# Where a latent attention phase places the gate-projection matmuls that fill its heads

## The reference

```python
q = split_heads(rms_norm(c_q, mla_cq_norm) @ mla_w_uq, MLA_HEADS)          # 8 heads
kv = split_heads(rms_norm(c_kv, mla_ckv_norm) @ mla_w_ukv, MLA_HEADS)
...
q = rms_norm(q, mla_q_norm)                      # per head and token
k = rms_norm(k, mla_k_norm)
... # rope on the last 32 of 96 columns
o_mla = merge_heads(block_causal_attention(q, k, v)) @ w_branch_mla
g_fox, g_mla = jnp.split(jax.nn.sigmoid(gate_logit + b_gate), N_BRANCH, axis=-1)
```

## Time and profile before

| | us |
|---|---|
| median of three runs | 2499.22 |
| the profiled execution | 2498.03 |
| span of its profile | 2496.2 |
| PE busy in the span | 2379.8 (95%) |
| DVE busy | 1411.5 (57%) |
| ACT busy | 960.2 (38%) |
| POOL busy | 505.1 (20%) |

### The profile page before, as it was taken

The page is one execution under the profiler, slowest core; times in us unless marked ns, Lnnn a source line. Parts: engine busy times, 40 slices in busy tenths (PEclk is TensorE's granted clock), DMA queues, the critical chain, the costliest instruction groups (busy, mean ns, idle before and its releaser), DMA issues. The chain is left out here.

```text
span 2496.2 us, 36863 instructions
## 1 busy us (share of the span) xinstructions
PE 2379.8 (95%) x14060; PEld 2108.6 (84%) x14060; DVE 1411.5 (57%) x2057; ACT 960.2 (38%) x1621; POOL 505.1 (20%) x632
## 2 busy tenths in 40 slices
PE   7999999999977999999999999989999999999999
PEld 7999999999977888887788888868877888887887
DVE  8665555665554674672555555454386666556553
ACT  6333333343333454453344333353343333333331
POOL 0033200000022432440233333332301232000000
PEclk8999999999988999989999999999999999999999
DMA  5366633375421000001111111034514665327553
GB/s 193 138 206 202 209 119 107 145 274 182 158 84 53 27 2 26 26 1 36 38 50 38 42 37 37 31 118 160 202 59 139 229 212 192 131 72 295 203 198 104
DMA packets 132698, 297.99 MB, mean 119 GB/s; under 512 B 10096, under 2 KB 57072, under 8 KB 129216
## 3 DMA queue, kind: packets, MB, share of 16 engines
q1 hardware_dynamic: 132544, 295.88, 34.1%
HBM read 206.99 MB, written 88.72 MB: 118 GB/s over the span
## 5 line engine op out<-in xcount | busy, mean ns | idle before, releaser
L1079 DVE TENSOR_TENSOR f_w_lo<-f_rw,f_w_hi 128x1024 fp32r<-128x1024 f32 x154 | 194.9, 1265 | 222.1 <-ACT f_w_hi L591 222.1
L842 PE MATMUL f_ps<-u_hi,f_w_hi 128*128 128x260 f32 (+1 forms) x1056 | 280.6, 320 | 10.6 <-DVE u_lo L1017 10.4
L842 PE MATMUL f_ps<-u_lo,f_w_hi 128*128 128x260 f32 (+1 forms) x1056 | 280.3, 320 | 0.0
L842 PE MATMUL f_ps<-u_hi,f_w_lo 128*128 128x260 f32 (+1 forms) x1056 | 279.9, 320 | 0.0
L842 PE MATMUL f_ps<-f_far_hi,f_w_hi 128*128 128x260 f32 (+1 forms) x792 | 214.3, 325 | 18.6 <-DVE f_ev L1095 8.8
L591 ACT CAST f_w_hi<-f_rw 128x1024 fp32r<-128x1024 f32 x154 | 160.9, 1046 | 163.5 <-PE f_ps L842 159.6
L842 PE MATMUL f_ps<-f_far_hi,f_w_lo 128*128 128x260 f32 (+1 forms) x792 | 213.0, 324 | 0.0
L842 PE MATMUL f_ps<-f_far_lo,f_w_hi 128*128 128x260 f32 (+1 forms) x792 | 212.7, 323 | 0.0
L842 PEld LDWEIGHTS f_ps<-u_hi,f_w_hi 128*128 128x128 f32 x1056 | 175.9, 190 | 26.0 <-issue 11.5
L842 PEld LDWEIGHTS f_ps<-u_lo,f_w_hi 128*128 128x128 f32 x1056 | 175.6, 189 | 14.0
L842 PEld LDWEIGHTS f_ps<-u_hi,f_w_lo 128*128 128x128 f32 x1056 | 175.7, 189 | 13.7
(11 more groups left out here) (392 smaller groups left out, 5964.1 us busy)
## 6 DMA issues: line engine op xcount, KB each, us to landing
f_rw<-in_gu SPq DMA_DIRECT2D x88, 512.0 KB, 4.2
f_rw<-kept_dsum SPq DMA_DIRECT2D x32, 704.0 KB, 4.4
f_rw<-kept_hid SPq DMA_DIRECT2D x33, 520.0 KB, 5.6
f_rw<-in_down SPq DMA_DIRECT2D x24, 704.0 KB, 4.2
f_rw<-kept_hid SPq DMA_DIRECT2D x33, 512.0 KB, 5.7
h_in<-in_wd SPq DMA_DIRECT2D x11, 1024.0 KB, 6.7
kept_dsum<-h_in SPq DMA_DIRECT2D x44, 256.0 KB, 2.9
h_out<-in_wd SPq DMA_DIRECT2D x11, 1024.0 KB, 7.3
```

Of the source, the lines that this page charges most:

```text
L842: last = nc.tensor.matmul(out[:, b, 0:N], w[:, c], u[:, b * N:(b + 1) * N], start=(j < 3 and k == 0 and i == 0), stop=(k == 3 and i == 2), ...
L1079: nc.vector.tensor_tensor(slot(w_lo, st), src, slot(w_hi, st).bitcast(F32), ALU.subtract).then_inc(wlo_done, 1)
```

## The change

Three tables and one condition change.

- `GROUPS`, used for the seven heads prepared beside another: place 1 of step 6 had 3 groups and has 1; place 0 of steps 8 and 9 had none and has 1 each.
- `FIRST`, the first head: place 1 of step 5 had 3 groups and has 1; place 0 of steps 11 and 13 had none and has 1 each. The copy of the last logit tile (`COPY_FIRST`) moves from step 12 to 13 with the last group.
- `first_roots`: the `split_lo` of the last unit comes in step 6 where it came in step 8.

```diff
         GROUPS = {(w, x): 1 for w in range(14) for x in range(2)}
-        GROUPS.update({(0, 1): 2, (1, 1): 2, (3, 1): 2, (4, 1): 2, (11, 1): 2, (12, 1): 2, (13, 0): 0, (13, 1): 0,
-                       (6, 1): 3, (8, 0): 0, (9, 0): 0})
+        GROUPS.update({(0, 1): 2, (1, 1): 2, (3, 1): 2, (4, 1): 2, (11, 1): 2, (12, 1): 2, (13, 0): 0, (13, 1): 0})
...
-        FIRST.update({(-1, 0): 1, (-1, 1): 4, (0, 0): 1, (0, 1): 2, (5, 0): 1, (5, 1): 3})
+        FIRST.update({(-1, 0): 1, (-1, 1): 4, (0, 0): 1, (0, 1): 2, (5, 0): 1, (5, 1): 1})
         FIRST.update({(w, x): 1 + 2 * x for w in range(1, 5) for x in range(2)})
-        FIRST.update({(w, 0): 1 for w in (8, 9, 10, 12)})
+        FIRST.update({(w, 0): 1 for w in range(8, 14)})
...
-        COPY_FIRST = (0, 2, 4, 12)
+        COPY_FIRST = (0, 2, 4, 13)
...
-                if 1 <= w < NU:
+                if 1 <= w <= NU:
                     split_lo(0, 0, w - 1)
-                if w == MAXIMA_FROM:
-                    split_lo(0, 0, NU - 1)
```

## The result

| | before | after |
|---|---|---|
| median, us (6 runs each) | 2499.53 | 2515.23 |
| range, us | 2498.03 to 2505.18 | 2508.69 to 2521.39 |
| profiled execution, us | 2498.03 | 2510.72 |
| its span, us | 2496.2 | 2508.9 |

The changed kernel is slower: ratio 1.0055, 95% interval 1.0039 to 1.0072, so about 14 us (15.7 between the medians). The direction was forecast, the size (7.7 us) was half of it, and the median lies above the range of 2500.5 to 2511.5.

The account below looks back on a forecast made before the run. PE, busy 95% of the span, was taken as the bound. Steady heads 6.3 us plus first head 1.4 made 7.7, giving 2505.7 on the profiled execution, 2506.9 on the median; forecast 2506.3 us, range 2500.5 to 2511.5.

Parts of the forecast that it names:

- Step 6 costs a wait of what left it: Steady heads, step 6: two groups leave, PE waits about 1.3 us for POOL's unchanged chain, step only 0.05 us earlier.
- The wait in step 9 goes: Steady heads, step 9: the arriving group covers the maxima tile's wait on DVE, gaining 0.44 us a head.
- Per steady head 0.90: Seven steady heads: 1.39 - 0.05 - 0.44 = 0.90 us more each, 6.3 us in all.
- The first head's order, 1.35: First head: 0.91 us from later DVE reductions plus 0.44 from the step 11 group delay transpose and next scores by 1.35.
- the forecast's 1209.56 and 1218.0: First head: predicted starts of the second wave of tiles, near 1209.56, and of the transpose, near 1218.0.
- The step 13 group: First head, step 13: the group lies in the 0.72 us wait before the transpose, costing nothing; 0.70 if uncovered.
- Rival 1: Steady heads, step 6: POOL's Newton steps finish sooner, so the sum is 1.5 to 4.6 us, about 2501.5; chance 0.10.
- Rival 2: Not slower: the chain into step 6's broadcast ends 1.24 us sooner; 2.9 us less than before, about 2495.7; chance 0.06.
- nothing is won or lost up to here: First head's last broadcast: it already waited 0.29 us for POOL; two groups fewer only lengthen that wait, at no cost.
- rival 3: Steady heads: PE's clock falls to 1.2 GHz after step 6's wait, about 3.5 us more each, 25 us, 2531; chance 0.04.
- its 0.91 us of order: First head: with `split_lo` ahead, DVE's maxima reductions start near 1209.22, 0.91 us later, and the delay runs through.

Follow-up runs that it names:

- both fillers: Changed kernel plus two unused product triples ahead of the first head's last broadcast and two ahead of its third maxima tile; 2507.31 us, ratio 1.0035.
- its filler: Changed kernel plus one unused triple ahead of the last head's first scores and one ahead of its first 512-column weighted sum; 2514.41 us, ratio 1.0057.
- once more: The changed kernel measured again with nothing altered; 2516.24 us, ratio 1.0059.
- first-head edits alone: Kernel before with only `FIRST`, `COPY_FIRST` and the early `split_lo` changed, old `GROUPS` kept; 2509.85 us, ratio 1.0038.
- late split: Changed kernel with `split_lo` of the last unit back in step 8 of the first head; 2511.3 us, ratio 1.0044.
- early split: Kernel before with only the earlier `split_lo` in the first head; 2506.73 us, ratio 1.0024.

## Why the prediction was half right

- **Step 6 costs a wait of what left it.** Right. 2.09 us of groups became 0.70 and a wait; the chain through POOL ends 1.90 us after its start, as before.
- **The wait in step 9 goes.** Right; the wait row is gone.
- **Per steady head 0.90.** Measured 0.95, and 1.07 at the last: 6 x 0.95 + 1.07 = 6.8 us against 6.3. The size was off by 0.5 us in all.
- **The first head's order, 1.35.** Right: 1.24 with both fillers. With the one ahead of the broadcast alone, where the row of tiles is untouched, the distance from broadcast to scores is 15.12 us against 13.79, 1.33 more. In that kernel the third tile starts 3.13 us behind the broadcast and the transpose 11.55; the forecast's 1209.56 and 1218.0 are 3.12 and 11.56 behind 1206.44. The step 13 group stayed covered.
- **Rival 1** did not happen (its "others took 0.20" holds for the earlier unit; in this one the first two steps take 0.43 and 0.39 in both kernels): the Newton step at 1310.51 is held to DVE's end, 0.64 us, and the 0.1 us between the two starts did not move. The rule of the Trainium skill ("SBUF — State Buffer", Who interferes with whom), by which the one that starts first holds the other up, agrees with this row too.
- **Rival 2** did not happen: the broadcast's chain was not shortened.
- **What failed** is the sentence on the first head: "two groups fewer ahead of it only lengthen that wait, so nothing is won or lost up to here". A longer wait was priced at nothing, and the clock behind it cost 4.7 us, in the form that rival 3 gave. The next term has the same gap: the early `split_lo` was priced at its 0.91 us of order, and alone it made the first head 5.1 us longer (50.33 against 45.27), although the broadcast's wait was the old one. Rival 3 was put in the wrong place. It was weighed for the steady heads, where PE then idles 1.1 us in one piece, 1.44 of 58 in all, and keeps 1.00, and given 0.04. The first head got no such test, though its waits were the ones to grow furthest, by 1.4 and 0.9 us within 4 us, on top of small ones left and right: from 1195 to 1230 PE was busy 32.02 of 35 us already in the kernel before. The evidence that the prediction quoted against rival 3 (2.20 us idle in 35 at a clock of 1.00) was of the first head as it was, and of its part ahead of these waits, not as the change would leave it.
- **What was missed altogether** is the clock in the last head, 4.6 us (52.67 against 48.08 with its filler).

The account: 6.8 for the steady heads, 1.2 for the first head's order, 4.7 and 4.6 for the clock, 17.3 of 17.4 us. Without the clock the forecast of 7.7 stands against 8.0: the terms for waits and order were right by their mechanism, and the missing 9.3 us are one thing, a clock that the sum held constant.

What stays open is, beside what decides at which wait the level falls, why the last head's low stretch hangs on the first head's. It is in all five profiles in which the first head lost 5 us or more and the last head has no filler (changed, once more, first-head edits alone, late split, early split), in none of the seven in which the first head lost at most 1.2 to the clock. The last head's own instructions are the same in all. That makes chance unlikely, but five profiles are few, and the stretch isn't one size: it costs about 4.6 us in three of them, 1.4 with the late `split_lo` and 2.0 with the early one alone, where it begins at the first of the two waits already (the scores' matmul behind it takes 0.71 us, not 0.50). What carries it over seven steady heads at 1.00 no run here shows.

## What to carry to other kernels

When a filling is moved from one place to another, price two things at the place it leaves: the wait that opens, and what PE's clock does behind it, above all where PE already waits at several points close together. Look there at the granted clock and at the distance between equal matmuls (0.23 or 0.43 us here) before the durations of anything else. And keep filling in front of a wait in a thin stretch, one where PE already waits at several points, even where it only fills: six unused matmuls ahead of one broadcast took the phase from 481.2 to 471.7 us here.

## What the runs showed of the hardware that was not expected

- In the first head, one or two waits of 1.5 to 1.7 us, with shorter ones around them, came in six profiles with a granted clock of 0.57 to 0.75 over the 20 us from the last broadcast; with unused matmuls in one of the two waits it was 1.00 and 0.91. In four of the six the broadcast right behind the first wait was at the lower level already (0.90 us for 0.54), in the changed kernel's first profile the fall came 3 us later at the second wait, and in one, without the first wait, 6 us behind the second. The wait of 1.1 us in step 6 of the steady heads was never followed by a fall. The Trainium skill ("TensorE: Matmul & The Clock Gate", A second HAM failure mode: psum-queue depth-cycling) tells of a kernel in which short idle times of PE between groups of matmuls made the clock swing between its two levels. These profiles agree: the lower level came with waits of 1.5 to 1.7 us in the first head, and in five of them with waits of 0.7 in the last.
- The low level costs less than its length says. 20 us at 0.66 do the work of 13.2, so 6.8 would be lost if PE had worked throughout; 4.7 were. Slower tiles wait less for DVE: 0.24 and 0.34 us, where the kernel with the filler ahead of the broadcast, in the same order at full clock, waits 0.43 and 0.56. That is 0.4 of the 2.1 us; the rest was not taken apart.
- In the last head, with the same instructions and the same two waits of 0.7 us, the low level came in five profiles and not in seven.
- The stages ahead of the phase, the same in all these kernels, took between 1174.60 and 1189.76 us, and 1174.60 and 1181.83 in the two profiles of the changed kernel. Distances inside the phase repeat to about 0.1 us where the clock is full.
